# A mixer kernel's opening, first attention sweep and gate activations rearranged: splits ahead of rounding, the value projection cut into units, the query rotation on another engine

## The chip, the cores and the metric

The kernel runs on one core of a Trainium2 chip. The metric is the device time of one execution in microseconds. A core has engines that run side by side, each in its own written order: PE (TensorE, matrix products and transposes, with PEld for its weight loads), DVE (VectorE), ACT (ScalarE), POOL (GpSimd) and SP (SyncE), which here only issues DMAs. They wait for each other through semaphores. PE writes to PSUM banks, the others read and write SBUF too.

## The reference, cut to what matters

```
def memory_attention(q, k, v):                      # 256 memory tokens, 4 heads
    p = softmax(einsum(q, k) * MEM_DIM ** -0.5);  return einsum(p, v)

def mla_mixer(c_q, c_kv, k_r, pos, q_norm, kv_norm, w_q_up, w_kv_up):   # 12 heads
    q = rms_norm(c_q, q_norm) @ w_q_up              # per head 64 "nope" + 32 "rope" columns
    q_nope, q_rope = q[..., :64], rope(q[..., 64:], pos)
    kv = rms_norm(c_kv, kv_norm) @ w_kv_up          # per head 64 of k, 64 of v
    k_rope = rope(k_r, pos)                         # one for all heads
    return causal attention(concat(q_nope, q_rope), concat(k_nope, k_rope), v)
...
# block A: h = x + norm(concat(mla_mixer, memory_attention) * silu(gate) @ w_out)
# block B: the same with a forget-gated attention in place of mla_mixer
# hybrid layer: a state space mixer (SSD) whose output y is multiplied by silu(z),
#               beside a stick-breaking attention
```

There are 512 tokens of width 1024 and 256 memory tokens; the memory is normalised once and projected to keys and values for blocks A and B. Everything is float32.

## The kernel before, in words

A float32 product is made of three PE products. Each operand is split into a high part, rounded to a format that PE takes at full rate, and a low part, the rest; PE adds high*high, high*low and low*high. Activations are split after the normalisation (acts_hi, acts_lo). Weights are split on their way in: they come in pieces of at most 128x1024 through four buffers (w_raw[p%4], DMAs on SP's queue); ACT makes the high part (high_part, L504), POOL subtracts it (rest, L509: w_lo = w_raw - w_hi), then PE multiplies (project_pe, L560), and ACT moves the result from its bank to SBUF (project_act, L588). There are two homes for a split piece, w_hi[p%2] and w_lo[p%2], so that piece q+2 is split only once the products of piece q are done (split_ahead_act, L513); some later pieces have homes of their own in w_more, named in `apart`.

The stages are written out by hand for each engine, and this written order is the only order. What the change touches, in the order of the run:

- **Opening.** The memory is normalised: square and root on ACT (L646, L649), the scaling on DVE (scalar_tensor_tensor, L687), the transposes on PE (L667), the rounding to acts_hi on ACT (L624), acts_lo on DVE (L705). keep_busy (L657) gives PE idle transposes meanwhile. Then p_mem[0] to p_mem[3] (keys and values of the memory for two blocks; 2 pieces each), with the normalisation of the four 128-token blocks of x between them, and pA_lat, the projection to the latents.
- **Block A's attention.** The latents are normalised and split (lat_high on ACT, lat_low on DVE). pA_qr makes the rotary part of the queries, DVE rotates it (rotate: L2194, L2196, L2197, 24 operations of 128x192), and signals rope_done. pA_v makes the values of all heads: 8 units (two halves of the heads by four token blocks) of six products of 128x384. Then the sweep (sweep_pe, sweep_act, sweep_dve) goes over 32 steps, four for each pair of heads: the first 8 steps are the memory's two pairs, the others the causal pairs. A step is score (PE, L825), maximum (DVE, L920), exp (ACT, L883), reciprocal and scaling (DVE, L926, L929), transposes (PE, L843), collecting (ACT, L894), values (PE, L857). In its gaps mla_pe puts project_head (L1113, the q and k columns of the next pair of heads) and turn_rope (L1099, the transposes of the rotated keys and queries, four turns in steps 4 to 7; the first query turn waits for rope_done); DVE copies out what was turned (L1181). The causal pairs' score(8) needs the last turn.
- **SSD.** The loop over heads has PE products of its own (L1552, L1564) and, beside them, the projection to z and v (beside_pe, L1473). ACT moves that out of its banks (L1491) and has the heads' Relu and Exp (L1434, L1436); for the first half of z the move is a Silu, and z_left is put through Silu behind it (L1494). DVE's att (L1682) is what L1564 multiplies. After the heads, ssd_gated (L1730, L1733) multiplies y by silu(z).

```
for S in (pA_qr, pA_v, pA_qk):
    project_pool(pool, S)
...
dve.wait_ge(lat_lo.sem, LATS)
dve.wait_ge(*pA_qr.evac(MB))
for m in range(MB):
    ...
    ins = rotate(x1, x2, x1, x2, b[0], b[1], [t[:, m * A_H:(m + 1) * A_H, :] for t in rot])
ins.then_inc(sem["rope_done"], 1)
mla_dve(dve)
```

That is the end of POOL's and DVE's programs ahead of block A's sweep. The functions that the diff touches:

## Time and profile before

| | |
|---|---|
| runs | 1229.39, 1231.12, 1233.16 us (median 1231.12) |
| profiled execution | 1233.21 us, of it 1231.5 us span from the first to the last instruction |
| mean granted TensorE clock in the span | 0.996 |
| busy share: PE, PEld | 98%, 76% |
| busy share: DVE, ACT, POOL | 44%, 48%, 34% |
| traffic | 100.99 MB, 82 GB/s mean |

A row of the timeline says when an instruction (or a run of xN like ones) started, how long it was busy, its engine and line, what it writes and reads; the bracket behind it is the idle time of that engine just before it and the instruction that ended the wait. The profiled execution is 2.1 us longer than the median of the three runs.

### The profile page before, as it was taken

Reading aid. Unit: us, or ns where it says so; the run is one execution under the profiler, and the core shown is the slowest. Engines: PE = TensorE matmul, PEld = TensorE weight load, DVE = VectorE, ACT = ScalarE, POOL = GpSimd, SP = SyncE. Lnnn points to the kernel's source line nnn. Section 1 sums busy time; section 2 is a strip of 40 time slices with the busy share of each in tenths; the row PEclk is TensorE's granted clock in tenths of the full one; section 3 lists DMA queues with packets and bytes.
Section 4 is the critical chain, followed back from the end, with each engine's and each line's share of the span. In section 5 each row is a group of like instructions: output and inputs, shape, how many; then the busy total and the mean of one; then the engine's idle time right before and its main releaser. Section 6 shows DMA issues by size and latency. Waiting matters only on the chain. (4 is left out here: it accounts for less than half of the span.)

```text
span 1231.5 us, 16504 instructions
## 1 busy us (share of the span) xinstructions
PE 1201.4 (98%) x6273; PEld 933.0 (76%) x6273; DVE 536.0 (44%) x996; ACT 593.5 (48%) x1247; POOL 415.6 (34%) x235
## 2 busy tenths in 40 slices
PE   8999989999999999999999999999999999999998
PEld 8988845568998666668888976787666667878886
DVE  4202555562410455552566644701776760032333
ACT  6345555554533555563554653534556552333242
POOL 5543401105254222225244323344222224444451
PEclk9999989999999999999999999999999999999999
DMA  8433201203134999813222412234111112323231
GB/s 290 122 105 78 64 18 33 69 18 99 58 120 93 61 94 61 123 52 88 70 86 62 127 52 69 69 88 116 53 53 52 52 52 86 103 86 103 86 103 68
DMA packets 111406, 100.99 MB, mean 82 GB/s; under 512 B 21140, under 2 KB 98272, under 8 KB 111328
## 3 DMA queue, kind: packets, MB, share of 16 engines
q1 hardware_dynamic: 108784, 95.35, 32.9%
q0 software_dynamic: 864, 3.15, 0.7%
q10 hardware_dynamic: 1680, 1.44, 0.4%
q8 instruction: 50, 0.82, 0.3%
q14 instruction: 28, 0.23, 0.1%
HBM read 94.68 MB, written 2.10 MB: 79 GB/s over the span
## 5 line engine op out<-in xcount | busy, mean ns | idle before, releaser
L509 POOL TENSOR_TENSOR w_lo<-w_raw,w_hi 128x1024 fp32r<-128x1024 f32 (+6 forms) x169 | 379.3, 2245 | 759.9 <-ACT w_hi L504 759.9
L504 ACT ACTIVATE w_hi<-w_raw 128x1024 fp32r<-128x1024 f32 (+6 forms) x169 | 167.7, 992 | 255.7 <-PE bank L560 228.4
L560 PE MATMUL bank<-acts_hi,w_hi 128*128 128x512 f32 (+1 forms) x592 | 228.9, 387 | 3.9 <-POOL w_lo L509 2.2
L560 PE MATMUL bank<-acts_lo,w_hi 128*128 128x512 f32 (+1 forms) x592 | 227.1, 384 | 0.0
L560 PE MATMUL bank<-acts_hi,w_lo 128*128 128x512 f32 (+1 forms) x592 | 227.0, 383 | 0.0
L560 PEld LDWEIGHTS bank<-acts_hi,w_hi 128*128 128x128 f32 x592 | 111.2, 188 | 28.7 <-issue 5.1
L560 PEld LDWEIGHTS bank<-acts_lo,w_hi 128*128 128x128 f32 x592 | 111.3, 188 | 22.2
L560 PEld LDWEIGHTS bank<-acts_hi,w_lo 128*128 128x128 f32 x592 | 111.3, 188 | 21.1
L560 PE MATMUL bank<-w_hi,acts_hi 128*128 128x512 f32 (+4 forms) x308 | 109.5, 356 | 4.0 <-POOL w_lo L509 1.7
L560 PE MATMUL bank<-w_hi,acts_lo 128*128 128x512 f32 (+4 forms) x308 | 108.6, 353 | 0.0
L560 PE MATMUL bank<-w_lo,acts_hi 128*128 128x512 f32 (+4 forms) x308 | 108.3, 352 | 0.0
L1924 DVE TENSOR_TENSOR_SCAN arena_end<-arena 128x512 f32<-128x512 f32 (+3 forms) x64 | 80.8, 1262 | 63.1 <-ACT arena L1872 63.1
L560 PEld LDWEIGHTS bank<-w_hi,acts_hi 128*128 128x128 f32 x308 | 57.9, 188 | 11.2 <-issue 2.3
L929 DVE TENSOR_SCALAR arena<-arena,stat 128x256 f32<-128x256 f32 (+3 forms) x128 | 64.3, 502 | 4.5
L894 ACT ACTIVATE arena<-bank 128x256 f32<-128x256 f32 (+3 forms) x128 | 47.0, 423 | 35.2 <-PE bank L843 35.1
L920 DVE TENSOR_REDUCE stat<-bank 128x1 f32<-128x256 f32 (+3 forms) x80 | 33.3, 458 | 70.3 <-PE bank L825 40.6
L560 PEld LDWEIGHTS bank<-w_hi,acts_lo 128*128 128x128 f32 x308 | 57.9, 188 | 6.0
L560 PEld LDWEIGHTS bank<-w_lo,acts_hi 128*128 128x128 f32 x308 | 58.0, 188 | 5.8
L883 ACT ACTIVATE arena<-bank,stat 128x256 f32<-128x256 f32 (+3 forms) x80 | 39.8, 505 | 41.1 <-DVE stat L920 41.1
L1782 PE MATMUL bank<-acts_hi,w_hi 128*128 128x512 f32 x144 | 58.5, 406 | 0.0
L1782 PE MATMUL bank<-acts_hi,w_lo 128*128 128x512 f32 x144 | 58.4, 406 | 0.0
L1782 PE MATMUL bank<-acts_lo,w_hi 128*128 128x512 f32 x144 | 57.6, 400 | 0.0
(275 smaller groups left out, 2044.9 us busy)
## 6 DMA issues: line engine op xcount, KB each, us to landing
w_raw<-in_w_in SPq DMA_DIRECT2D x64, 512.0 KB, 3.6
w_raw<-in_w_out SPq DMA_DIRECT2D x24, 512.0 KB, 3.6
w_raw<-in_w_in_b SPq DMA_DIRECT2D x22, 512.0 KB, 5.2
w_raw<-in_w_in_a SPq DMA_DIRECT2D x10, 512.0 KB, 3.8
w_raw<-in_w_mem_kv SPq DMA_DIRECT2D x8, 512.0 KB, 8.0
w_raw<-in_w_sb_proj SPq DMA_DIRECT2D x8, 512.0 KB, 3.4
w_raw<-in_w_ssd_proj SPq DMA_DIRECT2D x8, 512.0 KB, 3.5
arena_shared<-junk SPq DMA_DIRECT2D x11, 256.0 KB, 20.6
```

The costliest lines, as they stand in the source:

```text
L504: nc.scalar.activation(w_at(p)[0][:, 0:size], w_raw[p % RAW][:, 0:size], ACT.Copy).then_inc(w_high.sem, 1)
L509: nc.gpsimd.tensor_tensor(lo[:, 0:size], w_raw[p % RAW][:, 0:size], hi[:, 0:size].bitcast(F32), ALU.subtract).then_inc(w_rest.sem, 1)
L560: mm = nc.tensor.matmul(bank_of(S, s, g)[0:lhs.shape[1], 0:rhs.shape[1]], lhs, rhs, start=j + kk + t == 0, stop=j == len(S.pieces) - 1 and ...
L883: nc.scalar.activation(w2[i % 4][:, 0:n], src[:, 0:n], ACT.Exp, bias=stat[:, i % 8:i % 8 + 1], scale=-1.0 if X.less else 1.0, accum_out=st ...
L894: nc.scalar.activation(wT2[e][:, 0:blocks, b * P:(b + 1) * P], bank[6 + i % 2][:, 0:blocks * P].rearrange("p (c t) -> p c t", c=blocks), A ...
L920: nc.vector.tensor_reduce(stat[:, i % 8:i % 8 + 1], bank[2 + i % 4][:, 0:n], AX.X, ALU.max, negate=True).then_inc(A.lowest.sem, 1)
L929: nc.vector.tensor_scalar(w2[i % 4][:, 0:n], w2[i % 4][:, 0:n], stat[:, 16 + i % 8:17 + i % 8], None, ALU.mult).then_inc(A.weights.sem, 1)
L1782: mm = nc.tensor.matmul(qk_bank(q)[:, :], w[:, kk * P:(kk + 1) * P], acts[:, kk, :], start=x == 0, stop=x == 23)
L1924: nc.vector.tensor_tensor_scan(left[i % 2][:, T - n:T][:, ::-1], x, x, 1.0, ALU.mult, ALU.bypass).then_inc(sem["scan"], 1)
```

## The change

The order of the DMAs on SP stays. Four parts:

1. The opening. The memory's rows are scaled, turned and rounded in halves of 512 columns; the first piece of weights is made high ahead of the rounding, the second one behind it; p_mem[0]'s first piece waits only for the first half of the rows. Pieces 4 to 13 have four homes, so that their split waits for one piece less. PE does p_mem[2] directly behind p_mem[1], ahead of the transposes of x's last two blocks, whose banks are others. The latents' first piece takes the blocks in the order in which they were rounded (2, 3, 0, 1).
2. The value projection is no stage any more. Units 0 and 1 stand ahead of the sweep, the others in its steps 0, 1, 2, 3, 4 and 6, each behind turn_in; ACT stores units 0, 1, 6 and 7, DVE units 2 to 5. Its two pieces have homes of their own and are split as soon as the latents are rounded, and the first two pieces of pA_qk earlier too.
3. The rotation of the queries goes from DVE to POOL (rotate_q), behind the low parts of V's two pieces and of pA_qk's first two, and ahead of its third.
4. In the SSD's heads z leaves its bank by Copy; the eight Silus stand behind the heads.

```
+        FOUR_HOMES = range(4, 14)
+        apart = {p: (2048 * (p % 4) + 1536, 2048 * (p % 4) + 2560) for p in FOUR_HOMES if p % 4 < 2}
...
         def split_ahead_act(act, S, k, q):
-                act.wait_ge(C["product"].sem, S.done_after(k, q, S.groups - 1))
+                if S.piece0 + q + 2 in FOUR_HOMES:
+                    act.wait_ge(C["product"].sem, S.done_after(k, q - 1, S.groups - 1) if q else S.before)
+                else:
+                    act.wait_ge(C["product"].sem, S.done_after(k, q, S.groups - 1))
...
+        def rotate_q(pool, link):
+            pool.wait_ge(sem["rope_trig"], 1)
+            pool.wait_ge(*pA_qr.evac(MB))
+            for m in range(MB):
...
+                ins = rotate(nc.gpsimd, link, x1, x2, x1, x2, b[0], b[1], rot)
+                if m < MB - 1:
+                    link(ins)
+            ins.then_inc(sem["rope_done"], 1)
...
+        V_STEPS = (0, 1, 2, 3, 4, 6)
...
+            def v_unit(u):
+                c, g = u // MB, u % MB
...
+                if u >= 2:
+                    pe.wait_ge(*pA_v.evac(u))
+                if u == 7:
+                    pe.wait_ge(*attA.gated(1))
...
+            v_unit(0)
+            v_unit(1)
+            pe.wait_ge(*pA_qr.evac(MB))
+            sweep_pe(pe, attA, turn_in, counts, beside)
...
+                if n < 2 * MB:
+                    if n == 0:
+                        act.wait_ge(*pC_z.evac(2 * MB))
+                    z = (z_right[:, n // 2], z_left[n // 2])[n % 2]
+                    nc.scalar.activation(z, z, ACT.Silu).then_inc(sem["z_silu"], 1)
...
                         nc.scalar.activation(to, bank[ZB + g][:, 0:to.shape[1]],
-                                             ACT.Silu if c == 1 else ACT.Copy).then_inc(pC_z.evac.sem, 1)
-                    for g in range(MB) if c == 1 else ():
-                        nc.scalar.activation(z_left[g], z_left[g], ACT.Silu).then_inc(sem["z_silu"], 1)
+                                             ACT.Copy).then_inc(pC_z.evac.sem, 1)
...
             pool.dma_start(G_PRE[1], i["norm_pre"][1:2, :].partition_broadcast(P)).then_inc(gain_in.sem, 16)
-            for S in (pA_qr, pA_v, pA_qk):
-                project_pool(pool, S)
+            project_pool(pool, pA_qr)
+            project_pool(pool, pA_v)
+            rotate_q(pool, link)
+            project_pool(pool, pA_qk)
...
-            for m in range(MEMB):
-                round_act(act, pre_mem, m)
-                high_part(act, m, pieces[m][0] * pieces[m][1])
+            high_part(act, 0, pieces[0][0] * pieces[0][1])
+            for a, m in MEM_ORDER:
+                act.wait_ge(*pre_mem.turned(2 * m + a + 1))
+                hi, _, of = mem_part(a, m)
+                nc.scalar.activation(hi, of, ACT.Copy).then_inc(pre_mem.high_act.sem, 1)
+            high_part(act, 1, pieces[1][0] * pieces[1][1])
...
+            project_act(act, p_mem[1], first=middle_rows)
+            project_act(act, p_mem[2], first=lambda: norm_act_step(act, pre[0], 3, x_in_sem, rounds=False))
...
+            for n in range(2):
+                high_part(act, pA_v.piece0 + n, piece_size(pA_v, 0, n))
...
-            keep_busy(pe, 10, 7)
-            pe.wait_ge(*pre_mem.normed(2 * MEMB))
-            project_pe(pe, p_mem[0])
+                turn_mem(pe, m)
+            keep_busy(pe, 4, 7)
+            project_pe(pe, p_mem[0], ready=lambda n: pre_mem.normed(MEMB if n <= 4 else 2 * MEMB))
             norm_pe_step(pe, pre[0], 0)
             norm_pe_step(pe, pre[0], 1)
             project_pe(pe, p_mem[1])
+            project_pe(pe, p_mem[2])
             pe.wait_ge(*pre[0].normed(4))
+            pe.wait_ge(*p_mem[2].evac(2))
             norm_pe_step(pe, pre[0], 2)
             norm_pe_step(pe, pre[0], 3)
-            project_pe(pe, p_mem[2])
             project_pe(pe, p_mem[3])
-            project_pe(pe, pA_lat, pre[0])
+            project_pe(pe, pA_lat, pre[0], first_order=pre[0].order)
```

On ACT the opening stood so before, from the load of the gain for x to the first square of x (h is x's block; in the changed program all lines are shifted):

```order
L2095 DMA arena<-in_norm_pre 128x1024
L624 ACTIVATE acts_hi<-bank 128x4x128 x2
L504 ACTIVATE w_hi<-w_raw 128x1024
L624 ACTIVATE acts_hi<-bank 128x4x128 x2
L504 ACTIVATE w_hi<-w_raw 128x1024
L646 ACTIVATE junk,norm_stat<-h 128x1024
L649 ACTIVATE norm_stat<-norm_stat,eps_t 128x1
```

And the same place of ACT in the changed program (L510 is high_part, L2216 the rounding of the memory):

```order
L2211 DMA arena<-in_norm_pre 128x1024
L510 ACTIVATE w_hi<-w_raw 128x1024
L2216 ACTIVATE acts_hi<-bank 128x4x128 x4
L510 ACTIVATE w_hi<-w_raw 128x1024
L657 ACTIVATE junk,norm_stat<-h 128x1024
L660 ACTIVATE norm_stat<-norm_stat,eps_t 128x1
```

The first high part moved from between the roundings to ahead of all four, the second stays behind them.

On POOL, the end of its work ahead of the sweep, before (the 128x768 are pA_v's pieces, those of 384 and 256 columns pA_qk's):

```order
L2062 COPY arena<-arena 128x128 x4
L2065 DMA arena<-in_norm_pre 128x1024
L509 TENSOR_TENSOR w_lo<-w_raw,w_hi 128x768 x2
L509 TENSOR_TENSOR w_lo<-w_raw,w_hi 128x384
L509 TENSOR_TENSOR w_lo<-w_raw,w_hi 128x256
L509 TENSOR_TENSOR w_lo<-w_raw,w_hi 128x384
```

And in the changed program (the rotation is L1117 to L1120; its first of four blocks is shown whole):

```order
L2176 COPY arena<-arena 128x128 x4
L2179 DMA arena<-in_norm_pre 128x1024
L515 TENSOR_TENSOR w_more<-w_raw,w_more 128x768 x2
L515 TENSOR_TENSOR w_lo<-w_raw,w_hi 128x384
L515 TENSOR_TENSOR w_lo<-w_raw,w_hi 128x256
L1117 TENSOR_TENSOR arena_shared<-arena 128x192 x4
L1119 TENSOR_TENSOR arena<-arena_shared 128x12x16
L1120 TENSOR_TENSOR arena<-arena_shared 128x12x16
L1117 TENSOR_TENSOR arena_shared<-arena 128x192 x4
```

Four such blocks came in between pA_qk's second and third piece.

On PE, the first two steps of the sweep before (L825 score, L1113 project_head):

```order
L560 MATMUL bank<-w_hi,acts_lo 128x384
L825 MATMUL bank<-arena_end 128x256 x2
L1113 MATMUL bank<-acts_hi,w_hi 128x512
L1113 MATMUL bank<-acts_hi,w_lo 128x512
L1113 MATMUL bank<-acts_lo,w_hi 128x512
L1113 MATMUL bank<-acts_hi,w_hi 128x512
L1113 MATMUL bank<-acts_hi,w_lo 128x512
L825 MATMUL bank<-arena_end 128x256 x2
```

And in the changed program (L836 score, L1182 project_head, L1199 a unit of the values, six products in four rows):

```order
L836 MATMUL bank<-arena_end 128x256 x2
L1182 MATMUL bank<-acts_hi,w_hi 128x512
L1182 MATMUL bank<-acts_hi,w_lo 128x512
L1182 MATMUL bank<-acts_lo,w_hi 128x512
L1182 MATMUL bank<-acts_hi,w_hi 128x512
L1182 MATMUL bank<-acts_hi,w_lo 128x512
L1199 MATMUL bank<-w_more,acts_hi 128x384 x2
L1199 MATMUL bank<-w_more,acts_lo 128x384
L1199 MATMUL bank<-w_more,acts_hi 128x384 x2
L1199 MATMUL bank<-w_more,acts_lo 128x384
L836 MATMUL bank<-arena_end 128x256 x2
```

A unit stands between one score and the next; two more units stand ahead of the first score, in place of the eight of before.

## Rows read from the trace of the kernel before

**Rows 1.** The page: busy time of each engine, share of the span, instructions.

```profile
PE 1201.4 (98%) x6273; PEld 933.0 (76%) x6273; DVE 536.0 (44%) x996; ACT 593.5 (48%) x1247; POOL 415.6 (34%) x235
```

**Rows 2.** Timeline of the opening: start, busy us, engine, line, what, [idle before].

```profile
11.55 1.05 ACT L504 ACTIVATE w_hi<-w_raw 128x1024 fp32r<-128x1024 f32 x1
12.68 4.75 POOL L509 TENSOR_TENSOR w_lo<-w_raw,w_hi 128x1024 fp32r<-128x1024 f32 x2 [7.94 <-ACT w_hi L504]
15.20 0.36 PE L560 MATMUL bank<-acts_hi,w_hi 128*128 128x256 f32 x1 [0.41 <-POOL w_lo L509]
16.18 2.33 DVE L687 SCALAR_TENSOR_TENSOR hn<-h,norm_stat,arena 128x1024 f32<-128x1024 f32 x1
21.03 1.91 PE L667 MATMUL bank<-ident,hn 128*128 128x128 f32 x16
22.46 2.05 ACT L624 ACTIVATE acts_hi<-bank 128x512 fp32r<-128x512 f32 x4
22.70 0.36 PE L560 MATMUL bank<-w_hi,acts_hi 128*128 128x256 f32 x1
31.29 0.36 PE L560 MATMUL bank<-acts_hi,w_hi 128*128 128x256 f32 x1 [0.85 <-POOL w_lo L509]
38.09 0.36 PE L560 MATMUL bank<-w_hi,acts_hi 128*128 128x256 f32 x1 [0.82 <-POOL w_lo L509]
45.07 0.39 PE L560 MATMUL bank<-w_hi,acts_hi 128*128 128x336 f32 x1 [0.77 <-DVE acts_lo L705]
```

**Rows 3.** DMA view, the issue at 1.73: size, us to landing.

```profile
w_raw<-in_w_mem_kv SPq DMA_DIRECT2D x1, 512.0 KB, 7.7
```

**Rows 4.** Timeline from POOL's last load ahead of the sweep to score(8).

```profile
136.67 0.57 POOL L2065 DMA_DIRECT2D arena<-in_norm_pre  x1
138.34 1.82 POOL L509 TENSOR_TENSOR w_lo<-w_raw,w_hi 128x768 fp32r<-128x768 f32 x1 [1.11 <-ACT w_hi L504]
140.30 0.41 PE L560 MATMUL bank<-w_hi,acts_hi 128*128 128x384 f32 x1 [0.85 <-POOL w_lo L509]
149.47 0.70 PE L825 MATMUL bank<-arena_end 64*128 64x256 f32 x4 [0.58 <-ACT arena_shared L588]
162.22 0.66 PE L1099 MATMUL bank<-ident,arena 128*128 128x128 f32 x4 [0.68 <-DVE arena L1181]
171.35 1.22 PE L825 MATMUL bank<-arena 64*128 64x512 f32 x2 [1.52 <-issue]
```

**Rows 5.** Groups of POOL's and DVE's operations: count, busy, mean ns, idle before.

```profile
L509 POOL TENSOR_TENSOR w_lo<-w_raw,w_hi 128x384 fp32r<-128x384 f32 x7 | 7.2, 1035 | 47.7 <-ACT w_hi L504 47.7
L509 POOL TENSOR_TENSOR w_lo<-w_raw,w_hi 128x256 fp32r<-128x256 f32 x6 | 4.4, 726 | 37.6 <-ACT w_hi L504 37.6
...
L929 DVE TENSOR_SCALAR arena<-arena,stat 128x256 f32<-128x256 f32 x15 | 5.5, 366 | 0.5
```

**Rows 6.** Timeline: a scaling of DVE beside a subtraction of POOL.

```profile
240.78 2.35 POOL L509 TENSOR_TENSOR w_lo<-w_raw,w_hi 128x1024 fp32r<-128x1024 f32 x1 [5.92 <-ACT w_hi L504]
241.28 1.93 DVE L929 TENSOR_SCALAR arena<-arena,stat 128x128 f32<-128x128 f32 x1
```

**Rows 7.** Windows: us, PE PEld DVE ACT POOL busy, granted clock, DMA share, GB/s.

```profile
149.47:161.40 11.93, 10.41 (x59) 6.67 (x59) 8.36 (x31) 10.27 (x34) 2.46 (x3) 1.00 0.14 29
...
168.00:171.10 3.10, 1.09 (x8) 0.86 (x8) 2.73 (x9) 1.60 (x7) 0.00 (x0) 1.00 0.00 0
171.35:189.02 17.67, 17.66 (x83) 9.19 (x84) 7.23 (x21) 7.42 (x23) 1.00 (x1) 0.81 0.06 13
189.02:204.05 15.03, 15.03 (x92) 8.50 (x91) 8.37 (x26) 8.88 (x29) 1.73 (x2) 1.00 0.11 22
```

**Rows 8.** Timeline in the SSD's heads.

```profile
734.99 0.47 PE L1473 MATMUL bank<-w_hi,acts_hi 128*128 128x512 f32 x1 [1.07 <-ACT arena L1491]
739.83 1.28 ACT L1436 ACT_TABLE_LOAD   x1
742.53 1.10 PE L1564 MATMUL bank<-arena,arena_end 128*128 128x64 f32 x8 [1.56 <-DVE arena_end L1682]
```

More of the change, by code:

```diff
@@ L141, in __init__, with bank @@
         self.normed = normed
+    def bank(self, b0, m):
+        return self.places[m][b0 // 4] if isinstance(self.places[m], tuple) else b0 + self.places[m]
 class PostNorm:
@@ L299, in build @@
         akT2 = [cut(16384 + n * T, T) for n in range(2)]
-        a_v = cut(19968, MB, MAIN_W)
-        rot = [cut(3072 + n * 768, MB * A_H, HALF) for n in range(4)]
+        AV = MAIN_W // 2
+        a_v = [hn.rearrange("p a d -> p (a d)")[:, 0:MB * AV].rearrange("p (m n) -> p m n", m=MB),
+               cut(19968, MB, AV)]
+        rot = [cut(23296 + n * 192, A_H, HALF) for n in range(4)]
         mem_in = cut(19968, MEMB, D)
@@ L553, in emit @@
                     wh, wl = (w[:, 0:r * S.width].rearrange("p (k n) -> p k n", k=r) for w in w_at(p))
-                    for g in range(S.groups) if block is None else (block,):
+                    in_order = first_order if first_order and q == 0 else range(S.groups)
+                    for g in in_order if block is None else (block,):
                         if acts and isinstance(k, int) and k == 0 and q == 0:
@@ L589, in emit @@
                                              S.func).then_inc(S.evac.sem, 1)
-                split_ahead_act(act, S, k, s * len(S.pieces) + last)
+                if s * len(S.pieces) + last >= split:
+                    split_ahead_act(act, S, k, s * len(S.pieces) + last)
                 if between:
@@ L864, in sweep_pe @@
                 turn_in(before)
+                if beside:
+                    beside(s)
                 if s % 4 == 1:
@@ L1083, in build, with v_bank, store_v @@
         QKN = QN + KN
+        V_STEPS = (0, 1, 2, 3, 4, 6)
+        def v_bank(u):
+            return 6 + u if u < 2 else 1
+        def store_v(u):
+            return a_v[u // MB][:, u % MB, :], bank[v_bank(u)][:, 0:AV]
         def mla_pe(pe):
@@ L1116, in project_head, with beside @@
                     mm.then_inc(C["product"].sem, 1)
+            def v_unit(u):
+                c, g = u // MB, u % MB
+                if g == 0:
+                    pe.wait_ge(w_rest.sem, pA_v.piece0 + c + 1)
+                if u >= 2:
+                    pe.wait_ge(*pA_v.evac(u))
+                if u == 7:
+                    pe.wait_ge(*attA.gated(1))
+                wh, wl = (w[:, 0:2 * AV].rearrange("p (k n) -> p k n", k=2) for w in w_at(pA_v.piece0 + c))
+                for x in range(6):
+                    kk, t = x // 3, x % 3
+                    mm = nc.tensor.matmul(bank[v_bank(u)][:, 0:AV],
+                                          (acts_hi, acts_hi, acts_lo)[t][:, Q_LORA // P + kk, g * P:(g + 1) * P],
+                                          (wh, wl, wh)[t][:, kk, :], start=x == 0, stop=x == 5)
+                mm.then_inc(v_made.sem, 1)
+            def beside(s):
+                if s in V_STEPS:
+                    v_unit(2 + V_STEPS.index(s))
             def turn_in(n):
@@ L1169, in after, with between, keep_v @@
                     gated_high(act, attA, s - last - 1)
-            sweep_act(act, attA, lambda s: None, after)
+            def between(s):
+                if s in V_STEPS[4:]:
+                    keep_v(2 + V_STEPS.index(s))
+            def keep_v(u):
+                to, of = store_v(u)
+                act.wait_ge(v_made.sem, u + 1)
+                nc.scalar.activation(to, of, ACT.Copy).then_inc(pA_v.evac.sem, 1)
+            keep_v(0)
+            keep_v(1)
+            sweep_act(act, attA, between, after)
             for c in range(4, len(attA.pairs)):
@@ L1993, in gates_dve @@
             low_rows(dve, 1, gate_row, "m_hi", "m_lo")
+        for n, at in enumerate((0, 3072)):
+            apart[pA_v.piece0 + n] = (at, at + 2 * AV)
         for S in (pA_out, pB_out, pC_out):
@@ L2131, in _ @@
             project_act(act, pA_gate, between=lambda s: between_gate_act(act, s), freed=lambda j: lat_high(act, j))
-            project_act(act, pA_qr)
-            project_act(act, pA_v)
+            for n in range(2):
+                high_part(act, pA_v.piece0 + n, piece_size(pA_v, 0, n))
+            act.wait_ge(C["product"].sem, pA_qr.done_after(0, 0, MB - 1))
+            high_part(act, pA_qk.piece0, piece_size(pA_qk, 0, 0))
+            project_act(act, pA_qr, split=2)
+            high_part(act, pA_qk.piece0 + 1, piece_size(pA_qk, 0, 1))
             mla_act(act)
@@ L2157, in _ @@
             dve.wait_ge(consts.sem, 1)
-            norm_dve(dve, pre_mem)
+            scale_mem(dve)
+            for n, (a, m) in enumerate(MEM_ORDER):
+                hi, lo, of = mem_part(a, m)
+                dve.wait_ge(*pre_mem.high_act(n + 1))
+                nc.vector.tensor_tensor(lo, of, hi.bitcast(F32), ALU.subtract).then_inc(pre_mem.normed.sem, 1)
             norm_scale(dve, pre[0], 0)
@@ L2255, in _ @@
             pe.wait_ge(lat_lo.sem, LATS)
-            project_pe(pe, pA_v)
-            pe.wait_ge(*pA_v.evac(2 * MB))
             mla_pe(pe)
```

93 lines of the change are left out of this document (58 added, 35 removed).

## The prediction

> **What bounds it now.** I read the page first: PE is busy for 98% of the span, the others for less than half of it [rows 1]. So only what PE waits for, and the clock that it is granted, can move the time. Next came PE's waits, and at each place that the diff touches the timeline. In the opening PE stands still ahead of the second, third and fourth projection for 0.85, 0.82 and 0.77 us, and its first real product starts at 15.20, when POOL has the low part of the first weights [rows 2]. Ahead of block A's sweep it waits 0.85 for pA_v's low part and 0.58 for the last bank of the values; in the sweep it waits at the first query turn and, longest, 1.52 ahead of score(8) [rows 4]. By the windows the causal steps behind score(8) ran at a granted clock of 0.81 where the next ones had 1.00 [rows 7]. In the SSD's heads two idle times of 1.07 and 1.56 remain [rows 8]. Everything else in the diff moves work between engines that are not the bound.
>
> **The opening.** The first weights land at 1.73 + 7.7 = 9.4 [rows 3]. Their high part (1.05) was made at 11.55, behind the rounding of the memory's first block; now it is ahead of all four roundings: 10.5. The low part is half of POOL's 4.75, so 2.4 [rows 2]: 12.9 in place of 15.1. PE may start there, as the first half of the rows is rounded by about then. The second piece: four roundings of about 0.5 (four took 2.05 at 22.46) and the high part, 13.7 at the latest; low part 16.1; PE is through the first piece at 12.9 + 2.9 = 15.8 (half of the 5.8 from 15.20 to 21.03), waits 0.3 and ends at 19.0. The third piece is not so early, because POOL's next operations collide with DVE's scaling of x (2.33 at 16.18) and its weights land late; I put its low part at 21.0, where p_mem[1] now starts in place of 22.70: 1.7 gained. The three waits of 0.85, 0.82 and 0.77 should go, because the split of piece q+2 no longer waits for piece q: 2.4. Against that stand two new waits. ACT now has, ahead of p_mem[2]'s second split, the four roundings of x's first blocks (2.05) and a square of about the length of a high part; I count the square, 1.05, as late; and PE waits for p_mem[2]'s banks to be emptied ahead of the transposes of blocks 0 and 1, for which I put about half of one of the waits above: 0.45. Sum **−2.6**. If both new waits are covered it is −4.1; if the earlier start brings nothing, since landings set the third piece, −0.9.
>
> **The value projection.** pA_qr ends where the idle time of 0.85 began, at 139.45 [rows 4]. Two units (six products at 0.178, 1.07 each: the eight units took the 8.6 us from 140.30 to the idle 0.58 before 149.47) bring score(0) to 141.6, 7.9 earlier, and both waits go if V's low parts are ready; POOL is free at 136.67 + 0.57 = 137.2, so at 139.1 and 140.9, the first of them in time. The six other units are paid for in the sweep: in the 11.93 us from score(0) to the first query turn PE was busy for 10.41 [rows 7]; five units make that 15.8 with no idle time left, or 16.5 with the half of it that other engines still cause. PE then comes to the query turn at 157.4 to 158.1 (162.22 before). The sixth falls into the idle time behind it. The stores are off the path: one for each unit, shared between DVE and ACT, which in that window were busy for 8.36 and 10.27 of the 11.93 us [rows 7]; a store that is late delays only the next unit.
>
> **The rotation.** This is the step whose price no row shows: 24 operations of 128x192 with two inputs on POOL. The nearest rows are its subtractions: 726 ns at 256 columns, 1035 at 384 [rows 5], and 2.35 at 1024 [rows 6]; the line through 256 and 1024 gives 0.585 at 192. I take that; 0.73 as the upper end (no cheaper than 256 columns), 0.5 as the lower. POOL's start is 140.9 plus the low parts of pA_qk's first two pieces, 1.0 and 0.73: 142.6. Behind it 24 x 0.585 = 14.0, so 156.6. In that time some ten scalings of DVE (366 ns, [rows 5]) fall, and they may hold POOL up: beside a subtraction of POOL one such scaling took 1.93 in place of 0.366, it ended only with POOL's operation [rows 6], so the two engines exclude each other. At 0.25 for each of the ten, 2.5: the rotation ends at 159.1. PE waits some 1 to 2 us there, and what follows keeps its 9.13 us (162.22 to 171.35): score(8) at 168.2 to 168.3, **−3.0**. If POOL is never waited for, score(8) comes at 157.4 + 9.1 = 166.5: −4.8. At 0.73, with the full 0.366 for each, it ends at 142.6 + 17.5 + 3.7 = 163.8, score(8) at 172.9: +1.6. Queued behind the rotation on POOL is pA_qk's third piece, first needed behind the query turns (its own waits were for ACT, [rows 5]): nothing.
>
> The Trainium skill, page "SBUF — State Buffer", section "Who interferes with whom", says that DVE and GpSimd share one pair of ports under an exclusive lock, and that the loser blocks fully for the whole instruction of the other. The row of 1.93 agrees with it. By that rule each of the ten scalings would cost POOL its whole 0.366, 3.7 in place of 2.5; the rotation would end at 160.3 and the sum below would be 1.2 worse, 1222.5.
>
> **The clock.** The first causal pair took 17.67 us at a mean clock of 0.81, the next 15.03 at 1.00 [rows 7], for the same work but for a few products. At 0.81, with 1.2 GHz as the lower level, 0.19 x 2 x 17.67 = 6.7 us were spent on it, half of which, 3.4, is lost. Just ahead of it PE was busy for only 1.09 of 3.10 us [rows 7]. In the changed kernel the steps ahead of score(8) hold one more unit and less idle time, and the whole sweep is denser. I forecast that the level holds: 17.67 − 15.03 = **−2.6**; at least 0, at most −3.4.
>
> **The SSD.** ACT's load of another table stood twice in the loop (Silu, and Exp again: 1.28 at 739.83 [rows 8]), with the Silus; PE's 1.07 and 1.56 are what they cost. Both go: **−2.6**; if some other wait of 0.6 stays, −2.0; with the restart of the pipeline, −2.9. The eight Silus behind the heads cost nothing: ACT is idle there, and DVE asks for them tens of us later.
>
> **The sum.** −2.6 − 3.0 − 2.6 − 2.6 = −10.8. The profiled execution took 1233.21, the three runs have a median of 1231.12, and no row tells where the 2.1 between them lie; the median of all four is 1232.1, from which I subtract: **1221.3**. All lower bounds together (−4.1 − 4.8 − 3.4 − 2.9) give 1216.9, all upper ones (−0.9 + 1.6 + 0 − 2.0) give 1230.8.
>
> **The rivals.** (A) The clock falls all the same: PE now waits 1 to 2 us at the query turn and still at score(8), where DVE's copies of the turned rows and ACT's exps are a chain of their own. For it speaks that 1.52 ahead of score(8) is not touched by any edit; against it that far more work lies ahead. Then the 2.6 stay: 1223.9. (B) The other side: POOL becomes the bound of the sweep. At 0.73 an operation the rotation ends at 163.8, the clock gives nothing back, and the time is 1232.1 − 2.6 + 1.6 − 2.6 = 1228.5. At 1.0, the price of twice the columns [rows 5], it ends at 142.6 + 24.0 + 3.7 = 170.3, score(8) at 179.4, 8 late: 1234.9, slower; the step from gain to loss lies at 0.8 to 0.85. For it speaks that 16-column pieces of rows, with a broadcast factor, are a harder pattern than the contiguous subtractions; against it that nothing on POOL shows a cost of pattern. (C) The opening does not do what the diff says: landings and ACT's long list set its pace, and only 0.9 comes of it: 1223.0. The waits of 0.8 went with POOL's low part, and POOL can't start before ACT and the landings; that speaks for it, but ACT's own list had room ahead of those splits, whose release by PE was what came last, and that speaks against.
>
> **Chances.** My forecast 0.50, A 0.20, C 0.12, B 0.18, of which 0.05 is still faster, 0.08 lies in between and 0.05 is slower. Faster by over 0.3% (3.7 us, about what a measurement of this kernel tells from no change; under 1227.4) is 0.50 + 0.20 + 0.12 + 0.05 = 0.87, the same 0.08, slower 0.05. The likeliest case's own range is 1218.5 to 1223.5; the range for all, without B's upper half and the corner of all lower bounds, is 1217.0 to 1227.0.
>
> **What would show it.** In the changed kernel's timeline: the first product at about 12.9, p_mem[1] at 21.0, the latents at about 42.5 in place of 45.07, no wait for POOL ahead of p_mem[2] and p_mem[3]. The rotation's operations on POOL at some 0.585 each and its end at 159.1 − 2.6 = 156.5 (all that lies behind the opening comes 2.6 earlier); score(0) at 149.47 − 7.9 − 2.6 = 139.0, and score(8) at 171.35 − 3.0 − 2.6 = 165.7. A granted clock of 1.00 for the first causal pair. No table load in the SSD's heads and no idle time over 0.6 at their projections. The forecast is wrong if the rotation takes over 0.73 an operation, if PE waits over 3 us at the query turn, or if a stage behind the sweep, which no edit touches, has got longer.

## The result and the profile after

The changed kernel takes 1221.43 us in the median of 5 executions (1220.76 to 1224.90), the kernel before 1231.34 (1229.39 to 1233.16): a ratio of 0.9925, interval 0.9906 to 0.9943. The forecast was 1221.3. The profiled execution took 1220.76 us, 12.45 less than the profiled one of before; the medians are 9.9 apart, and why these two differ is what the experiments had to find.

The page of the changed kernel, its span and the busy time of each engine:

```profile
span 1219.0 us, 16491 instructions
PE 1195.6 (98%) x6261; PEld 931.1 (76%) x6261; DVE 535.0 (44%) x978; ACT 592.5 (49%) x1246; POOL 429.7 (35%) x259
```

PE is still the bound. Its timeline in the changed kernel, at the places of [rows 2] and [rows 4]; L570 are the projections, L678 the transposes of x, L836 the scores, L1168 the turns:

```profile
13.65 0.36 PE L570 MATMUL bank<-acts_hi,w_hi 128*128 128x256 f32 x1 [0.17 <-DVE acts_lo L2286]
17.24 0.39 PE L570 MATMUL bank<-acts_hi,w_hi 128*128 128x256 f32 x1 [0.49 <-POOL w_lo L515]
21.97 0.39 PE L570 MATMUL bank<-w_hi,acts_hi 128*128 128x256 f32 x1
31.87 0.50 PE L570 MATMUL bank<-acts_hi,w_more 128*128 128x256 f32 x2 [1.05 <-POOL w_more L515]
35.38 1.94 PE L678 MATMUL bank<-ident,hn 128*128 128x128 f32 x16 [0.52 <-issue]
42.90 0.47 PE L570 MATMUL bank<-w_more,acts_hi 128*128 128x336 f32 x2
...
139.05 0.70 PE L836 MATMUL bank<-arena_end 64*128 64x256 f32 x4
...
155.67 0.66 PE L1168 MATMUL bank<-ident,arena 128*128 128x128 f32 x4
159.59 0.66 PE L1168 MATMUL bank<-ident,arena 128*128 128x128 f32 x4 [0.17 <-DVE arena L1290]
...
165.17 1.13 PE L836 MATMUL bank<-arena 64*128 64x512 f32 x4 [1.79 <-issue]
```

Read against the rows of before: the first product 15.20 to 13.65, p_mem[1] 22.70 to 21.97, the latents 45.07 to 42.90 without a wait, score(0) 149.47 to 139.05, the first query turn 162.22 to 155.67, also without a wait, score(8) 171.35 to 165.17. The two new waits of the opening are there, 1.05 and 0.52. The wait ahead of score(8) has grown from 1.52 to 1.79.

The wait of 1.05 has an origin on ACT. Its written order puts the two stores of p_mem[1] ahead of the high part of p_mem[2]'s second piece, and for the second store it waited for PE until 28.03:

```profile
28.03 0.38 ACT L598 ACTIVATE arena_end<-bank 128x256 f32<-128x256 f32 x1 [1.05 <-PE bank L570]
28.31 1.05 ACT L510 ACTIVATE w_more<-w_raw 128x1024 fp32r<-128x1024 f32 x1
```

POOL's part in it, from the timeline: V's and pA_qk's low parts, and the last block of the rotation (L1117, L1119, L1120):

```profile
134.80 3.64 POOL L515 TENSOR_TENSOR w_more<-w_raw,w_more 128x768 fp32r<-128x768 f32 x2
138.40 1.68 POOL L515 TENSOR_TENSOR w_lo<-w_raw,w_hi 128x384 fp32r<-128x384 f32 x2
140.06 2.27 POOL L1117 TENSOR_TENSOR arena_shared<-arena 128x192 f32<-128x192 f32 x4
...
153.47 0.60 POOL L1119 TENSOR_TENSOR arena<-arena_shared 128x192 f32<-128x192 f32 x1
154.03 0.68 POOL L1120 TENSOR_TENSOR arena<-arena_shared 128x192 f32<-128x192 f32 x1
```

The rotation takes 14.65 us, from 140.06 to 154.71, and is done 0.96 ahead of PE's turn. What runs beside it is paid by DVE: the scalings (L942) by DVE's summary for 140 to 156, and for 156 to 165, when POOL is through (the numbers behind the count are shortest, median and longest in ns):

```profile
L942 DVE TENSOR_SCALAR arena<-arena,stat x10: 353/499/765, 141.8 to 154.4; 128x256 f32<-128x256 f32 x10
...
L942 DVE TENSOR_SCALAR arena<-arena,stat x6: 353/354/356, 157.0 to 164.1; 128x256 f32<-128x256 f32 x6
```

The clock, by windows of the changed kernel (columns as in [rows 7]), the first causal pair and the next:

```profile
165.17:180.00 14.83, 14.83 (x85) 8.18 (x87) 7.43 (x21) 7.44 (x23) 1.22 (x2) 1.00 0.07 14
180.00:195.00 15.00, 15.00 (x93) 8.48 (x93) 8.36 (x25) 8.85 (x29) 1.69 (x3) 1.00 0.11 23
```

The next pair's first score starts at 179.76, so the first window holds 0.24 us of that pair: the pair that took 17.67 at 0.81 takes 14.59 at 1.00. In the SSD's heads ACT's timeline shows z's four Copies between two Exps and no table load, and PE's has no idle time from 720 to 735:

```profile
723.01 0.63 ACT L1545 ACTIVATE arena_end<-arena_end 128x512 f32<-128x512 f32 x1
723.55 2.04 ACT L1605 ACTIVATE arena<-bank 128x512 f32<-128x512 f32 x4
725.46 1.08 ACT L510 ACTIVATE w_hi<-w_raw 128x1024 fp32r<-128x1024 f32 x1
726.40 0.62 ACT L1543 ACTIVATE arena_end<-bank 128x512 f32<-128x512 f32 x1
```

Instruction by instruction, PE's lead over the kernel before is 2.17 at the latents' first product, 6.18 at score(8), 9.27 at the next score (179.35 has become 170.08), 9.3 up to the SSD's heads, and 12.3 behind them (742.53 has become 730.21). So in these two executions the opening gave 2.2, the values and the rotation some 3.7 to 4.0 (4.0 between the two profiles; 3.7 by the experiments below), the clock 3.1, the heads 3.0.

### The profile page after: what moved, and what is told of

It reads as the page before. It is cut to its first block and busy times, and to the rows that moved or that the text cites. A ratio compares the mean times of both kernels' runs of the same rounds, so it can differ in the third digit from the quotient of the medians.

```text
span 1219.0 us, 16491 instructions
## 1 busy us (share of the span) xinstructions
PE 1195.6 (98%) x6261; PEld 931.1 (76%) x6261; DVE 535.0 (44%) x978; ACT 592.5 (49%) x1246; POOL 429.7 (35%) x259
## 5 line engine op out<-in xcount | busy, mean ns | idle before, releaser
L515 POOL TENSOR_TENSOR w_lo<-w_raw,w_hi 128x1024 fp32r<-128x1024 f32 (+6 forms) x161 | 362.5, 2252 | 718.6 <-ACT w_hi L510 718.6
L510 ACT ACTIVATE w_hi<-w_raw 128x1024 fp32r<-128x1024 f32 (+6 forms) x161 | 159.9, 994 | 236.1 <-PE bank L570 212.3
L570 PE MATMUL bank<-acts_hi,w_hi 128*128 128x512 f32 (+1 forms) x576 | 224.7, 390 | 3.2 <-DVE acts_lo L2057 1.6
L570 PE MATMUL bank<-acts_lo,w_hi 128*128 128x512 f32 (+1 forms) x576 | 222.9, 387 | 0.0
L570 PE MATMUL bank<-acts_hi,w_lo 128*128 128x512 f32 (+1 forms) x576 | 222.8, 387 | 0.0
L570 PEld LDWEIGHTS bank<-acts_hi,w_hi 128*128 128x128 f32 x576 | 108.3, 188 | 27.9 <-issue 3.8
L570 PEld LDWEIGHTS bank<-acts_lo,w_hi 128*128 128x128 f32 x576 | 108.2, 188 | 22.0
L570 PEld LDWEIGHTS bank<-acts_hi,w_lo 128*128 128x128 f32 x576 | 108.3, 188 | 21.2
L570 PE MATMUL bank<-w_hi,acts_hi 128*128 128x512 f32 (+4 forms) x248 | 90.0, 363 | 1.6 <-DVE arena L950 1.6
L570 PE MATMUL bank<-w_hi,acts_lo 128*128 128x512 f32 (+4 forms) x248 | 89.4, 361 | 0.0
L570 PE MATMUL bank<-w_lo,acts_hi 128*128 128x512 f32 (+4 forms) x248 | 89.2, 360 | 0.0
L570 PE MATMUL bank<-w_more,acts_hi 128*128 128x512 f32 (+3 forms) x296 | 75.4, 341 | 0.0
L942 DVE TENSOR_SCALAR arena<-arena,stat 128x256 f32<-128x256 f32 (+3 forms) x128 | 65.7, 513 | 4.5
L515 POOL TENSOR_TENSOR w_more<-w_raw,w_more 128x1024 fp32r<-128x1024 f32 (+4 forms) x21 | 43.5, 2085 | 43.5 <-ACT w_more L510 43.4
L570 PEld LDWEIGHTS bank<-w_more,acts_hi 128*128 128x128 f32 x296 | 51.6, 189 | 3.8
```

Source lines behind the costliest of these rows:

```text
L510: nc.scalar.activation(w_at(p)[0][:, 0:size], w_raw[p % RAW][:, 0:size], ACT.Copy).then_inc(w_high.sem, 1)
L515: nc.gpsimd.tensor_tensor(lo[:, 0:size], w_raw[p % RAW][:, 0:size], hi[:, 0:size].bitcast(F32), ALU.subtract).then_inc(w_rest.sem, 1)
L570: mm = nc.tensor.matmul(bank_of(S, s, g)[0:lhs.shape[1], 0:rhs.shape[1]], lhs, rhs, start=j + kk + t == 0, stop=j == len(S.pieces) - 1 and ...
L942: nc.vector.tensor_scalar(w2[i % 4][:, 0:n], w2[i % 4][:, 0:n], stat[:, 16 + i % 8:17 + i % 8], None, ALU.mult).then_inc(A.weights.sem, 1)
```

## The experiments

**Each part alone.** Three kernels are the one before with one part of the diff each: ssd_only (part 4), open_only (part 1), sweep_only (parts 2 and 3). The fourth, b_busy, leaves the work as before and only fills PE's idle time ahead of step 7's turn and ahead of score(8):

```
+                if fill and s == 8:
+                    keep_busy(pe, 11, 1)
                 score(s)
                 before, after = counts(s)
+                if fill and s == 7:
+                    pe.wait_ge(*A.gated(1))
+                    keep_busy(pe, 6, 1)
                 turn_in(before)
```

Expected of ssd_only:

> The kernel before with the fourth part alone (z by Copy, the Silus behind the heads). Theory: the parts add up, and PE's two idle times of 1.07 and 1.56 us in the heads go with their restarts, so 2.6 to 3.1 us faster than before, about 1228.5. Rival: the time is only moved to a later wait of the hybrid layer, and the kernel is within 0.8 us of before.

Expected of open_only:

> The kernel before with the first part alone (the opening). Theory: the latents start 2.2 us earlier and all behind them keeps its pace, so 2.0 to 2.4 us faster, about 1229.1, with the first causal pair still at a low mean clock. Rival: the earlier start is given back at a later transfer, 0 to 0.8 us faster.

Expected of sweep_only:

> The kernel before with the second and third part (the values in units, the rotation on POOL). Theory: score(8) comes 3.7 us earlier in the span, and the first causal pair runs at full clock, another 3.0: 6.7 us faster, about 1224.6. Rival: the clock of that pair has to do with what the opening does and falls all the same: 3.7 us faster, about 1227.6.

Expected of b_busy:

> The kernel before with idle products of 128x128 put on PE ahead of the turn of step 7 (six) and ahead of score(8) (eleven), where it waits for 0.87 and 1.52 us. The result is not touched. Theory: the low clock of the first causal pair follows from PE's idle time ahead of it, so the pair takes about 15.0 in place of 17.7 us and the kernel is 2.5 to 3 us faster, about 1228.5, with score(8) at the same time. Rival: the clock falls for another reason, and the kernel is within 0.5 us of before, with a mean clock of about 0.81 in that pair.

Measured, each against 32 executions of the kernel before: ssd_only 1227.30 us (ratio 0.9965, 0.9953 to 0.9978), open_only 1230.16 (0.9985, 0.9973 to 0.9998), sweep_only 1227.60 (0.9966, 0.9955 to 0.9978), b_busy 1231.18 (0.9988, 0.9978 to 0.9998), before 1232.10. The medians alone hide what happened; the single executions with their mean granted clock show it:

| kernel | executions, us (mean granted clock) |
|---|---|
| before, 32 | 3 at 1229.5 (0.999 to 1.000); 13 at 1231.0 to 1231.5 (0.998); 6 at 1232.7 to 1233.4 (0.996); 10 at 1234.4 to 1234.8 (0.994) |
| ssd_only, 12 | 7 at 1226.3 to 1227.9 (0.998 to 1.000); 5 at 1229.7 to 1230.0 (0.996) |
| open_only, 12 | 7 at 1228.0 to 1230.2 (0.998, 0.999); 5 at 1231.7 to 1233.0 (0.994 to 0.996) |
| sweep_only, 9 | 8 at 1227.4 to 1229.0 (0.997, 0.998); 1 at 1229.5 (0.996) |
| b_busy, 12 | 12 at 1230.8 to 1231.8 (0.998 to 1.000) |

The kernel before has four levels, and the profiles tell something of what lies between them. The profile of before is one of the third level: its clock falls behind score(8) [rows 7] and nowhere else. The profile of ssd_only, whose sweep is that of before, has no fall there; the same stretch by windows:

```profile
171.10:188.80 17.70, 17.70 (x99) 9.33 (x96) 9.41 (x27) 9.20 (x29) 1.72 (x2) 1.00 0.09 20
```

PE waits the same 1.52 us ahead of score(8) in this execution, the clock stays at 1.00, and 17.7 us hold 99 of PE's instructions in place of 83; the pair takes 14.59 (170.73 to 185.32). So the fall in the sweep is no fixed part of the kernel: the same waits bring it in one execution and not in another. The profile of sweep_only shows a second place. It keeps the Silu of before, and PE's timeline and the windows in the SSD's heads read:

```profile
727.77 0.47 PE L1546 MATMUL bank<-w_hi,acts_hi 128*128 128x512 f32 x1 [1.07 <-ACT arena L1564]
735.31 1.10 PE L1637 MATMUL bank<-arena,arena_end 128*128 128x64 f32 x8 [1.56 <-DVE arena_end L1755]
...
740.44 1.00 PE L1637 MATMUL bank<-arena,arena_end 128*128 128x64 f32 x8
```

```profile
728.00:735.00 7.00, 5.75 (x29) 4.17 (x28) 0.50 (x2) 6.97 (x12) 2.38 (x1) 1.00 0.00 0
735.00:745.00 10.00, 9.69 (x48) 7.79 (x48) 4.81 (x8) 4.05 (x7) 2.36 (x1) 0.83 0.36 105
```

Behind the wait of 1.56 the clock falls too; PE loses 1.6 us there (5.13 from 735.31 to the next products of this line, 3.54 in the profile of before, from 742.53 to 746.07). Its 1227.6 is the number of the rival, but not for the rival's reason: the first causal pair is at full clock in the profile, and what is missing went in the heads.

With a step of about 1.7 for the heads and 3.5 for the sweep the four levels would be neither, the heads, the sweep, and both (1229.5, 1231.2, 1233.0, 1234.7). This reading is an inference from two profiles and the sums, and it is not shown. For it speaks that ssd_only, without the heads' waits, has two groups in place of four levels, with one execution between them. Two profiles speak against it. open_only's has a short fall in the sweep: its next score comes 6.47 us behind score(8), where ssd_only's needs 4.92 and before's 8.00, and the 1.6 lost would make the same second level. And b_busy, below, keeps the heads' waits without a fall there (3.55 between its two rows):

```profile
168.54 1.13 PE L833 MATMUL bank<-arena 64*128 64x512 f32 x4 [1.52 <-issue]
175.01 0.49 PE L833 MATMUL bank<-arena 64*128 64x128 f32 x4
```

```profile
740.53 1.10 PE L1569 MATMUL bank<-arena,arena_end 128*128 128x64 f32 x8 [1.56 <-DVE arena_end L1687]
744.08 1.00 PE L1569 MATMUL bank<-arena,arena_end 128*128 128x64 f32 x8
```

No execution of b_busy lies more than 1.0 above its lowest, so that a step of 1.6 for the heads is in none of the 12. What the second and the fourth level are stays open.

b_busy shows that the fall in the sweep goes when the idle time ahead of it is filled. In its timeline the filler runs up to score(8), and the windows of the same stretches as above are

```profile
169.90 2.62 PE L657 MATMUL bank<-tri_le,ident 128*128 128x128 f32 x22
172.45 1.13 PE L825 MATMUL bank<-arena 64*128 64x512 f32 x4
```

```profile
168.50:172.45 3.95, 3.95 (x38) 3.83 (x36) 2.17 (x7) 1.68 (x6) 0.00 (x0) 1.00 0.00 0
172.45:187.50 15.05, 15.05 (x86) 8.22 (x87) 7.41 (x21) 7.65 (x25) 1.44 (x2) 1.00 0.07 15
```

Its filler was too long by 1.3 us (23.20 from score(0) to score(8), 21.88 before), so that it is no faster than the good executions of before (1229.5 and 1.3 make 1230.8, its lowest); the expectation of 1228.5 had missed that. But none of its 12 executions is at 0.996 or below, against 16 of 32 of before.

Where the clock holds, ssd_only is 3.2 us below before (1226.3 and 1229.5), about as expected; the medians are 4.8 apart, since fewer of its executions have a fall. open_only and sweep_only have no execution at 1.000. PE's lead in their profiles ahead of the first fall is 2.5 at the latents and 2.8 at score(8) in open_only, and 4.2 at score(8) in sweep_only; but 0.5 of these 4.2 are there at the latents already (44.61 against 45.07), up to where sweep_only is the kernel before. So parts 2 and 3 give 3.7, and the opening of one program does not take the same time in each execution; more on that below.

**The changed kernel with one thing undone or made worse.** rope_dve puts the rotation back on DVE ahead of its sweep; pad1 and pad4 do the four products of the first block, or of all four, twice; no_four takes the four homes away:

```
-            rotate_q(pool, link)
+            rotate_q(dve, link)            # rope_dve: on DVE, ahead of mla_dve
...
+                if m in (0,):              # pad1; pad4: (0, 1, 2, 3)
+                    for n, (x, f) in enumerate(((x1, b[0]), (x2, b[1]), (x2, b[0]), (x1, b[1]))):
+                        ins = nc.gpsimd.tensor_tensor(rot[n], x, f, ALU.mult)
+                    link(ins)
...
-        FOUR_HOMES = range(4, 14)
+        FOUR_HOMES = range(0)              # no_four
```

Expected of rope_dve:

> The changed kernel with the rotation of the queries back on DVE, ahead of its part of the sweep. Theory: the units of the values in the sweep pay only because DVE is free for the first maximum; with 24 operations of about 0.45 us ahead of it that maximum comes some 9 us later, score(8) 6 to 8 us later, and the first causal pair may lose its clock again: 1227 to 1232. Rival: the gain is that of the values in PE's gaps, and the place of the rotation hardly matters: 1221 to 1223.

Expected of pad1:

> The changed kernel with the four products of the first block's rotation done twice on POOL (one chain link more), 2.4 us more work there. The result is not touched. Theory: POOL is only 1.0 us ahead of PE at the first query turn, so that the turn comes 1.4 us later and score(8) 0.6 to 1.4: 1222 to 1223. Rival: the steps of the sweep have slack behind the turn, and nothing changes: within 0.4 us of the changed kernel.

Expected of pad4:

> The changed kernel with the four products done twice in all four blocks, 9.6 us more work on POOL, as if an operation took 0.95 us in place of 0.59. The result is not touched. Theory (the rival of the other side in the forecast): the rotation ends at about 164.3, the first query turn 8.7 us later than now, score(8) about 8, and PE stands idle long enough for the clock to fall (3 more): 1229 to 1232.5. Rival: PE has other work to do meanwhile and loses under 4 us: below 1225.5.

Expected of no_four:

> The changed kernel with pieces 4 to 13 in two homes again, so that their split waits for one piece more. Theory: the waits for POOL's low part ahead of p_mem[2], p_mem[3] and the latents come back, and the latents start 1 to 2.4 us later: 1222.4 to 1224. Rival: the other edits of the opening give the gain: within 0.4 us of the changed kernel.

Measured: rope_dve 1229.50 (ratio to before 0.998, 0.9968 to 0.9992), pad1 1224.82 (0.9943, 0.9921 to 0.9966), pad4 1231.53 (1.000, 0.999 to 1.001), no_four 1223.86 (0.9939, 0.992 to 0.9958). Three medians lie where their theory had them; pad1's lies 1.8 above its range of 1222 to 1223. In rope_dve's timeline DVE's first maximum comes behind the rotation, at 148.06 (139.87 in the changed kernel), and a unit of the values stands still until DVE has stored the one before it:

```profile
150.64 1.01 PE L1199 MATMUL bank<-w_more,acts_hi 128*128 128x384 f32 x2 [5.95 <-DVE hn L1286]
...
173.74 1.13 PE L836 MATMUL bank<-arena 64*128 64x512 f32 x4 [1.79 <-issue]
```

Behind the wait of 5.95 the clock is at 0.50 (150.64 to 155), and none of its executions is over 0.997. So parts 2 and 3 belong together: with the units in the gaps and the rotation on DVE, the whole change is worth 1.8 us. In pad1 PE's first query turn waits for POOL:

```profile
156.88 0.63 PE L1172 MATMUL bank<-ident,arena 128*128 128x128 f32 x4 [1.30 <-POOL arena L1120]
...
166.35 1.13 PE L836 MATMUL bank<-arena 64*128 64x512 f32 x4 [1.79 <-issue]
```

2.4 us more on POOL move that turn and score(8) by 1.2, about as the theory had it, so POOL's lead was about 1.2. Its median is higher by more, 3.4, because in its 4 executions the clock is 0.997 to 0.999 and in the profiled one it falls behind score(8). In pad4 the turn is at 164.99 behind a wait of 8.29, and no execution has a clock over 0.996; the fall comes behind that wait (0.67 from 165 to 170), and the causal pair is at full clock. This is the forecast's rival of the other side at an operation of 0.95 us, which brings the kernel back to the time of before and no further.

```profile
164.99 1.08 PE L1172 MATMUL bank<-ident,arena 128*128 128x128 f32 x4 [8.29 <-POOL arena L1120]
```

no_four has back PE's waits for POOL's low part and starts the latents at 45.65, 2.75 later:

```profile
28.88 0.35 PE L570 MATMUL bank<-acts_hi,w_hi 128*128 128x256 f32 x1 [0.83 <-POOL w_lo L515]
33.56 0.39 PE L570 MATMUL bank<-acts_hi,w_hi 128*128 128x256 f32 x1 [1.58 <-POOL w_lo L515]
45.65 0.39 PE L570 MATMUL bank<-w_hi,acts_hi 128*128 128x336 f32 x1 [0.74 <-issue]
```

It costs 2.4 in the median (its four executions lie at 1223.7 to 1224.4), and its latents start no earlier than those of before (45.07): without its homes the opening gives nothing.

**A version that is faster.** In all these profiles of the changed sweep score(8) waits 1.79 us, wherever the sweep begins: a chain, not a coincidence. DVE copies the last turned block out only behind a step's scalings; in the changed kernel that copy ends at 165.07, 0.1 ahead of score(8):

```profile
164.39 0.68 DVE L1290 TENSOR_SCALAR arena<-bank 128x512 f32<-128x512 f32 x1
```

`early` puts the copies of steps 5 to 7 ahead of them, and early7 also moves the last unit of the values to step 7:

```
                 lowest(2 * s + 1)
+                if early:
+                    early(s)               # keep_turned(s - 4) for s in 5, 6, 7
                 share(2 * s)
...
-        V_STEPS = (0, 1, 2, 3, 4, 6)
+        V_STEPS = (0, 1, 2, 3, 4, 7)       # early7 alone
```

Expected of early:

> The changed kernel with DVE's copies of the turned query rows (steps 5 to 7) between a step's maxima and its scalings, where DVE waits some 0.3 us for the exp, in place of behind the scalings. Theory: the 1.8 us that PE waits ahead of score(8) are the wait for the last copy, which now ends 1.0 to 1.3 us earlier: 1219.5 to 1220.4 where the clock holds, and fewer executions with a fall of the clock. Rival: the scalings come 0.4 us later in each of three steps, their transposes with them, and the gain is used up: within 0.4 us of the changed kernel.

Expected of early7:

> As the run before it, and the last unit of the values in step 7 in place of step 6. Theory: the unit fills part of PE's wait ahead of score(8), so score(8) comes 1.3 to 2.2 us earlier than in the changed kernel: 1218.6 to 1219.5 where the clock holds. Rival: the unit's store on ACT, now behind step 7's exps, holds up the collecting of the weights and the first causal scores: no faster than the changed kernel.

Measured: early 1219.62 (0.9881 of before, 0.9863 to 0.9899), early7 1220.07 (0.9885, 0.9867 to 0.9902). The seven executions of before beside them have a median of 1234.89, five of them at 0.994, so these two ratios say more than the change gives; the times are to be read against the changed kernel's. In early's timeline the copy ends at 163.59, and

```profile
162.91 0.68 DVE L1285 TENSOR_SCALAR arena<-bank 128x512 f32<-128x512 f32 x1
...
163.69 1.13 PE L836 MATMUL bank<-arena 64*128 64x512 f32 x4 [0.48 <-issue]
```

score(8) comes 1.5 us earlier and waits 0.48. In early7 it comes at the same 163.69, now behind ACT's store of the moved unit (a wait of 0.62): the further edit gained nothing. That is the rival's mechanism; the rival's time, no faster than the changed kernel, was not met, since the early copies are in early7 too. Once more, beside the changed kernel itself:

> The changed kernel once more, beside the next one on the same chip. Theory: its executions come in levels too, most at 1220.8 to 1222.1 and some at about 1224.9, where the clock falls ahead of the first causal pair; none shows the fall in the hybrid layer's heads. Rival: the one long execution was an accident, and all lie within 1 us.

> The version with DVE's early copies once more. Theory: 1.4 us less than the changed kernel beside it, from score(8) at 163.7 in place of 165.2, and fewer or no executions with the fall, since PE waits 0.6 in place of 1.95 us there. Rival: the two medians lie within 0.5 us of each other.

The changed kernel: 1221.49 in the median, with executions at 1220.5 to 1222.1 (0.998, 0.999) and two at 1225.0 and 1225.1 (0.996). early: 1219.65, 4 executions from 1219.1 to 1220.3, all at 0.999 or 1.000. The medians are 1.8 apart (1.4 expected), and 1.2 without the two long executions. The profile of this second look at the changed kernel is one with the fall, by windows:

```profile
162.50:165.50 3.00, 1.81 (x14) 1.16 (x12) 2.36 (x8) 2.36 (x9) 0.00 (x0) 1.00 0.00 0
165.50:171.50 6.00, 5.40 (x14) 2.34 (x15) 1.78 (x3) 0.64 (x2) 0.00 (x0) 0.59 0.00 0
```

One program, two executions: up to the causal scores PE's instructions lie within 0.9 us of the first profile, and behind them 4.1 later. The 0.9 come from the opening. ACT waits for a landing of weights there, and PE for the low part that is made of them:

```profile
24.40 1.06 ACT L510 ACTIVATE w_more<-w_raw 128x1024 fp32r<-128x1024 f32 x1 [3.28 <-DMA w_raw<-in_w_mem_kv]
...
32.76 0.50 PE L570 MATMUL bank<-acts_hi,w_more 128*128 128x256 f32 x2 [1.69 <-POOL w_more L515]
...
43.80 0.48 PE L570 MATMUL bank<-w_more,acts_hi 128*128 128x336 f32 x2
```

Of the nine profiles with this opening and its homes, five start the latents at 42.55 to 42.99 and four at 43.66 to 43.85; in three of these four ACT's wait of 3.27 to 3.48 is put down to such a landing. The four profiles with the opening of before start them at 44.41 to 45.07. The means are 43.22 and 44.73, so the opening is worth some 1.5 us, estimated from these thirteen profiles, and not the 2.2 of the first pair, in which before has the latest start of its four. open_only's fastest execution, 1228.0, is 1.5 below the fastest of before too.

No profile of the changed kernel shows a fall in the heads. In 11 executions of it the fall in the sweep was there three times, by their clock, in 8 of early never; that early is rid of it is likely, not shown.

## Why the prediction was right

The time was met (1221.3 and 1221.43), in part by luck: errors cancelled.

- **Opening**, −2.6 forecast, −2.2 measured between the two profiles and some −1.5 in the mean of all. The three old waits are gone, and no_four shows that the homes carry the gain. Mis-sized was the term of 1.7 for p_mem[1], which starts at 21.97 and not at 21.0: 0.73 gained. The first product was put at 12.9 and came at 13.15 to 13.74 in the ten profiles with this opening, no_four's among them. The step "PE may start there, as the first half of the rows is rounded by about then" left out DVE's low part of the rows, which ended last in seven of the ten; in three it was POOL's low part of the weights. The new waits have the forecast sizes (1.05 and 0.45; measured 1.05 and 0.52), but the first by luck: the forecast put the 1.05 down to a square on ACT, and in the profile after ACT is through with that square and waits for PE ahead of its stores; the split behind the stores is what PE waits for. In the second look at the same kernel the wait is 1.69.
- **Values and rotation**, −3.0 forecast, −3.7 to −4.0 measured. An operation of the rotation was put at 0.585 (the line through the two rows gives 0.591, 0.1 us more in all); it took 0.57 to 0.68 (14.65 us for 24 with their links). score(0) was forecast at 139.0 and came at 139.05. Mis-sized was the term of 2.5 for DVE's scalings holding POOL up: the rotation ended at 154.7 (156.5 forecast), PE did not wait, and DVE paid in its place (median 0.499 for a scaling beside POOL, 0.354 without). The Trainium skill, page "SBUF — State Buffer", section "Who interferes with whom", says that which of the two engines blocks is decided by issue order. No run here shows the order of issue itself; the trace shows DVE as the one that waited, and the sum by POOL's full 0.366 for each was the worse one.
- **Clock**, −2.6 forecast, −3.1 between the two profiles, since the first pair at full clock takes 14.59 and not the next one's 15.03. But this step failed as a statement on the kernel: I read the low clock of one execution as a fixed price of the first causal pair. The executions show a clock of 0.996 or less in half of before's (16 of 32), sweep_only's profile shows a second fall in the SSD's heads of 1.6 that was missed, and the changed kernel can still have the first. PE's idle time is the cause in the sense that the fall vanishes when the idle time ahead of score(8) is filled (b_busy), and that, by the clocks, a fall is there in every execution where a long wait is added (pad4 and rope_dve; in their profiles behind that wait and not in the causal pair). Why the same waits bring it in one execution and not in another stays open. Between the medians the clock accounts for about 1: 9.9, less the 8.7 between the lowest executions at 0.999 and over (1229.5 and 1220.8).
- **SSD**, −2.6 forecast, −3.0 measured, 3.2 for the part alone. The Silus behind the heads cost nothing visible.
- **The sum.** Without falls of the clock the parts give 9.2 between the two profiles, and 8.2 to 8.7 with the opening at its mean (1.5, 3.7 to 4.0, 3.0 to 3.2); 8.7 was measured between the lowest executions. The forecast took 10.8, with 2.6 for the clock, from 1232.1; this base, a median with falls in it, lies 2.6 above the executions without them, as much as the clock term took off again. The opening, forecast about 1 too large, and the values with the rotation, about 1 too small, cancelled too.
- **The rivals.** B's mechanism is real: pad4, at 0.95 for an operation, ends on before's time; POOL's lead is only 1 us. The forecast put the step from gain to loss at 0.8 to 0.85, but with its own terms (5.2 for the opening and the heads, and no clock) it comes out at 0.88. A (the fall stays, 1223.9) is what 3 of 11 executions show, at 1224.9 to 1225.1. C is there in part: in four of nine profiles the opening loses about 1.0 against the other five, in three of them behind a landing of weights, and what is left of it in the mean, 1.5, lies between C's 0.9 and the forecast's 2.6.

## What to carry to other kernels

When executions of one program differ in steps of a few us, list them with their granted clock before a stretch of low clock in one profile is entered into a sum; it may be an accident of that execution, and its price belongs to a chance. The same holds for a gain that is read off one pair of profiles: the opening's 2.2 was 1.5 over more of them. Moving work into PE's gaps paid here only with the engine relieved that the gaps wait for, and then the next chain (here a copy queued behind two scalings) was worth a look: reordering one engine gave 1.8 us more in the median, 1.5 of it at score(8). A resource with a lead of 1 us is not free for more work.

## What was not expected of the hardware

The clock. In windows behind PE's idle times it read 0.50 to 0.59 on average, at or near the lower of its two levels, and in other executions of the same program, with the same waits ahead, 1.00. The times of before fall into four groups, 1229.5 to 1234.8, and their mean clocks into the same order, 1.000 to 0.994. In b_busy PE was busy for all of the 3.95 us ahead of the causal scores (168.50 to 172.45), the clock was 1.00 there and behind, and none of its 12 executions had a mean clock under 0.998; the filler cost 1.3 us, and the times lie within 1.0 us.

DVE and POOL slowed each other unequally: beside the rotation DVE's scalings went from 0.354 to a median of 0.499, and POOL's operations stayed at 0.57 to 0.68. And a rotation with 16-column pieces and a broadcast factor costs POOL no more than the line through its contiguous subtractions says (0.59).
